# Attention loop of a hybrid transformer layer: the last two value tiles of a step behind the latent scores, and a pair's two copies behind the high halves of groups 0 and 1

## The reference

```python
def block_attention(q, k, v):
    ...
    def one_block(qi):
        s = jnp.einsum('bkgqd,bksd->bkgqs', qi, kt).astype(jnp.float32) * scale
        p = jax.nn.softmax(s, axis=-1).astype(vt.dtype)
        return jnp.einsum('bkgqs,bksd->bkgqd', p, vt)

    o = lax.map(one_block, qb)
    return o.transpose(1, 0, 4, 2, 3, 5).reshape(B, T, Hq * hd)

def reference(x, c, ctx, ...):
        ...
        attn_lat = block_attention(q_lat, jnp.concatenate([k_lat, k_ctx], axis=1),
                                   jnp.concatenate([v_lat, v_ctx], axis=1))
```

## Time and profile before

| | |
|---|---|
| time before, median of 3 runs | 2780.42 us (2778.55 to 2780.79) |
| the profiled execution | 2782.8 us, its span 2781.0 us |
| PE busy over the span | 2698.0 us, 97% |
| DVE busy | 1482.7 us, 53% |
| ACT busy | 627.9 us, 23% |
| POOL busy | 541.7 us, 19% |

### The profile page before, as it was taken

The page is one execution under the profiler, slowest core; times in us unless marked ns, Lnnn a source line. Parts: engine busy times, 40 slices in busy tenths (PEclk is TensorE's granted clock), DMA queues, the critical chain, the costliest instruction groups (busy, mean ns, idle before and its releaser), DMA issues.

```text
span 2781.0 us, 35088 instructions
## 1 busy us (share of the span) xinstructions
PE 2698.0 (97%) x14088; PEld 2202.9 (79%) x14088; DVE 1482.7 (53%) x2349; ACT 627.9 (23%) x1152; POOL 541.7 (19%) x468
## 2 busy tenths in 40 slices
PE   8999999999999999999999989999999999999998
PEld 3888888888888867877777777777778888888887
DVE  6645444344443474167655688867444444444444
ACT  4200000000000044243345688851110000000002
POOL 0065456465420000005420032220000000000001
PEclk9999999999999999999999999999999999999999
DMA  8112112222211122111233100025201111111112
GB/s 294 38 65 65 61 57 73 87 87 91 91 47 37 40 85 66 50 57 62 84 116 107 63 1 1 16 84 161 82 24 53 45 45 53 45 46 52 45 45 76
DMA packets 198289, 187.67 MB, mean 67 GB/s; under 512 B 7645, under 2 KB 149770, under 8 KB 198026
## 3 DMA queue, kind: packets, MB, share of 16 engines
q1 hardware_dynamic: 190160, 171.83, 19.4%
q10 hardware_dynamic: 7994, 13.97, 1.3%
HBM read 161.39 MB, written 24.38 MB: 67 GB/s over the span
## 4 chain that ended last, share of the span: by engine, by line
PE 86%; DVE 6%; ACT 4%; issue 2%; DMA 1%; ACTq 0%; POOL 0%; DVEq 0%; SPq 0%
PE psum L221 26%; PE psum L222 25%; PE psum L223 25%; DVE ptl L1995 2%; PE psum L1876 1%; ACT pth L1945 1%; PE psum L314 1%; ACT prob L1928 1%; PE psum L1500 1%; PE psum L1894 1%; PE psum L1893 1%; PE psum L408 1%; DVE wl L198 1%; PE psum L570 0%; DMA raw<-in_w_out_dram 0%
## 5 line engine op out<-in xcount | busy, mean ns | idle before, releaser
L221 PE MATMUL psum<-nh,wh 128*128 128x512 f32 (+2 forms) x1688 | 627.7, 372 | 1.4 <-DVE wl L198 1.4
L222 PE MATMUL psum<-nl,wh 128*128 128x512 f32 (+2 forms) x1688 | 613.8, 364 | 0.0
L223 PE MATMUL psum<-nh,wl 128*128 128x512 f32 (+2 forms) x1688 | 613.3, 363 | 0.0
L814 ACT ACTIVATE silu_a<-psum 128x512 f32<-128x512 f32 (+1 forms) x110 | 61.2, 556 | 1494.2 <-PE psum L223 1494.2
L196 DVE CAST wh<-raw 128x1024 fp32r<-128x1024 f32 (+1 forms) x173 | 122.4, 708 | 492.9 <-PE psum L223 492.8
L221 PEld LDWEIGHTS psum<-nh,wh 128*128 128x128 f32 (+1 forms) x1688 | 317.3, 188 | 65.9 <-issue 7.1
L222 PEld LDWEIGHTS psum<-nl,wh 128*128 128x128 f32 (+1 forms) x1688 | 317.2, 188 | 52.7 <-issue 4.1
L223 PEld LDWEIGHTS psum<-nh,wl 128*128 128x128 f32 (+1 forms) x1688 | 316.8, 188 | 52.3
L846 DVE SCALAR_TENSOR_TENSOR h<-psum,gates,h 128x512 f32<-128x512 f32 (+1 forms) x400 | 270.9, 695 | 155.9 <-PE psum L223 153.7
L221 PE MATMUL psum<-hidh,wh 128*128 128x512 f32 (+1 forms) x880 | 331.3, 376 | 11.1 <-DVE hidl L830 7.6
L222 PE MATMUL psum<-hidl,wh 128*128 128x512 f32 (+1 forms) x880 | 326.7, 371 | 0.0
(11 more groups left out here) (258 smaller groups left out, 3769.1 us busy)
## 6 DMA issues: line engine op xcount, KB each, us to landing
raw<-in_w_ffn_up_dram SPq DMA_DIRECT2D x88, 512.0 KB, 3.9
mod_part<-in_w_mod_dram SPq DMA_DIRECT2D x96, 256.0 KB, 4.2
raw<-in_w_ffn_down_dram SPq DMA_DIRECT2D x44, 512.0 KB, 3.7
raw<-in_w_in_dram SPq DMA_DIRECT2D x34, 512.0 KB, 3.9
mod_raw<-in_w_mod_dram SPq DMA_DIRECT2D x12, 1024.0 KB, 13.9
gates_saved<-staged ACTq DMA_DIRECT2D x40, 256.0 KB, 2.0
merge_gate<-gates_saved SPq DMA_DIRECT2D x8, 1024.0 KB, 5.2
x_rows<-in_x_dram SPq DMA_DIRECT2D x8, 512.0 KB, 8.1
```

The lines of the kernel that those rows point to most:

```text
L221: pe.matmul(o, hi_w, hi_x, start=first, stop=False)
L222: pe.matmul(o, hi_w, lo_x, start=False, stop=False)
L223: return pe.matmul(o, lo_w, hi_x, start=False, stop=last)
L814: nc.scalar.activation(silu_a[:, c, 0:w], ps[c][:, 0:w], ACT.Silu).then_inc(self.a_free, 1)
```

## The change

On PE, the five value tiles of a step are split in three and two. The first three stay where they were; the last two come behind the latent scores. On ACT, the fold of a pair (in an odd i) comes behind the high halves of groups 0 and 1, no longer ahead of them. No instruction is added or removed, and no wait is written anew.

```diff
             if i >= 4:
 
-                values((i - 4) // 2, range(5, K_TILES) if i % 2 else range(0, 5))
+                tiles = range(5, K_TILES) if i % 2 else range(0, 5)
+                values((i - 4) // 2, tiles[0:3])
             if 2 <= i <= N_STEP:
                 turn(i - 1, (0, 1))
             if i + 2 < N_STEP:
                 score(i + 2, False)
+            if i >= 4:
+                values((i - 4) // 2, tiles[3:5])
             if i in EARLY_MERGE:
...
             if 1 <= i < N_STEP:
                 exp_latent(act, i)
+            if 1 <= i <= N_STEP:
+                high(i - 1, (0, 1))
             if i >= 5 and i % 2 == 1:
                 fold((i - 5) // 2)
-            if 1 <= i <= N_STEP:
-                high(i - 1, (0, 1))
```

## The result

The changed kernel takes 2834.01 us, median of 4 runs (2832.33 to 2834.72), against 2780.61 us for the one before, run beside it (2778.55 to 2781.5). The ratio is 1.0192 with a 95% interval of 1.0175 to 1.021: 53 us slower. The forecast was 2838 us, 41 of it from a new wait and 17 from PE's clock.

What follows compares the result with a forecast made beforehand. A ring of waits among three nearly full engines, PE, DVE and ACT, was taken to set the time. 2780.4 + 41 (new wait) + 17 (PE's clock) = 2838 us; range 2814 to 2862.

Steps and rivals of the forecast that it cites:

- The wait: Odd step, ACT: a new pair's first high half waits for `pv_done`, now behind the latent scores; idle 1.8 us.
- The walk: Odd step, timed from the x2: high half at +3.80 instead of +2.82, DVE's finish at +5.59, 1.42 us later.
- third rival: Odd step: ACT's high halves start at once, only the fold waits; 0.45 us a pair, 2793 us; chance 0.05.
- What a pair costs: Attention steps: a pair takes 9.76 us instead of 8.34, 1.42 more; 29 pairs make 41 us.
- The clock: PE's new idle times halve its clock in 12 of 29 pairs (two in five), 1.4 us each, 17 us; chance 0.52.
- DVE decides: Even step: DVE reaches its low half 1.96 us behind its maxima, at +8.93, later than the high half allows (+8.80).
- the tie with PE: End of the even step: PE is free at +9.76, just when the next x2 follows DVE's low half.
- the clock stays up: PE's clock never falls in the attention steps: 2821.6 us, down to 2816; chance 0.25.
- the clock falls for long: PE's low stretches last 6.7 us: 40 us in place of 17, 2862 us; chance 0.13.
- the high half isn't held: Odd step: ACT's wait is for an earlier pair, so only the fold is held; 13 us, 2793 us; chance 0.05.
- No change: Attention steps: a gain of some 0.3 us a pair against a loss of the same size; chance 0.02.
- Faster: Odd step: earlier transposes save DVE's 0.32 us wait and the new wait is free; 9 us, 2771 us; chance 0.03.

Runs made afterwards that it cites:

- three_buffers: The changed kernel with a third buffer of the turned probabilities for the pairs 0 to 14; 2811.57 us, ratio 1.0124.
- filled: The changed kernel, with the latent scores of odd steps computed a second time behind the value tiles, only then raising their semaphore; 2824.51 us, ratio 1.0167.
- odd_split: The kernel before with ACT's new order and only the odd steps' value tiles split three and two, even steps unsplit; 2835.59 us, ratio 1.0195.
- pe_only: The kernel before with only the PE part of the change, ACT's fold still ahead of the high halves; 2832.85 us, ratio 1.0184.
- odd_one_tile: As odd_split, but with one value tile instead of two behind the latent scores in odd steps; 2836.23 us, ratio 1.0204.
- even_split: The kernel before with only the even steps' value tiles split three and two, ACT in its old order; 2778.39 us, ratio 0.9991.
- rb_behind_even: The kernel before with even steps split three and two, and only the fold's copy of the reciprocals behind the high halves; 2770.04 us, ratio 0.9971.

## Why the prediction was right

By its steps, with the odd step above; +0 is the x2 at 1702.84.

- **The wait.** The high half is released by the value matmul L1894, after 1.75 us (1.8 forecast). three_buffers shows that it is the buffer's wait and not something else at that place.
- **The walk.** The exponential is read out at +1.99 (+1.98), the high half starts at +3.73 (+3.80), DVE's low half at +4.36 (+4.42), the finish at +5.51 (+5.59), the x2 at +5.20 (+5.26), the context scores at +6.12 (+6.23). The last value matmul ends at +3.70 (1706.26 + 0.28), as forecast; ACT follows it by 0.03 and not by 0.10, and with that each later step is a little early. The idle times of PE are 1.50 and 0.51 to 0.66 (1.56 and 0.56). A pair takes 9.6 to 9.8 us (9.76). The releaser is L1894 in the changed kernel too; the prediction called it L1897, but the lines added to the file stand behind it. In its third rival 1704.18 is +3.12, not +3.15, which changes nothing.
- **What a pair costs.** 1.42 forecast; before, pairs were 8.2 to 8.35 us, as the one shown in the earlier trace rows, and are now 9.65 to 9.8: 1.43 more, each kind against its like. In all, without the clock, 52.0 - 13 = 39 us against the 41 of the sum. The difference lies at the loop's end, which the prediction put at nothing: by the distances of filled, which has no fall, the first 28 are 40.9 us longer than before, and the last three, where no latent scores are left, 1.3 us shorter (the last but one 8.30 in place of 9.93).
- **The clock.** Nine falls, each 3.4 us long, against twelve at 3.5; 1.0 to 1.6 us each, pair by pair against filled, 1.4 in the mean as forecast; 12.4 to 13.5 us together against 17. That the clock would fall in part of the pairs and not in all was the weakest step, a choice between bounds of 0 and 40. No row gave the two in five, and kernels with idle times as long or longer had four to six falls in as many pairs (odd_split, pe_only, odd_one_tile), so that nine came near to twelve is partly luck. filled shows that the idle times are the cause, and that the falls have a price.
- **A length that was wrong without harm.** "DVE decides" in the even step rested on 1.96 us as DVE's own length. It was 1.78 (even_split). In the changed kernel the tie with PE, which the prediction also found, holds the step at the same place. In the next pair, at full clock, the low half is at 1722.80, +8.82 in place of +8.93, and PE goes on without an idle time from its value matmuls to the x2, 9.76 us behind that at 1713.98:

```profile
1723.74 0.38 PE L1876 MATMUL psum<-cst,prob 128*128 128x128 f32 x2
```

Of the rivals, *the clock stays up* fell with nine low stretches in the trace, *the clock falls for long* with their length, 3.4 us and not 6.7, *the high half isn't held* with the releaser; what it priced at 0.45 a pair is close to what the first pairs of three_buffers show, 0.33 to 0.49 in most. *No change* fell with the time. *Faster* was right in what ACT and DVE had to give: rb_behind_even collects it, with `pv_done` left where it was.

## What to carry to other kernels

Before moving the work that raises a semaphore, list every wait on that semaphore, those that guard a buffer too: here the visible consumer was moved along, and the costly one was the guard of a double buffer two pairs on, written in another function. A split can be right in one half of a pair and wrong in the other, so try the halves apart. And where a ring of three nearly full engines sets the time, a saving on one of them counts only once the other two can follow; of the two edits that gave 9 us together, neither moved the median alone by more than the measurement can tell, though the even split had shortened the attention steps by 4.7 us in the trace.

## What the runs showed of the hardware that I had not expected

The clock fell in every third pair, with the same idle times of PE (1.50, and 0.51 to 0.66 us behind it) in the two pairs between, where it stayed full. Each fall lasted 3.4 us. The longest idle time is a poor guide. One of 2.81 us had left the clock full before, while in even_split it fell behind one of 1.74 us at the same place of the kernel. At the start of the attention steps it fell behind 2.09 us before and stayed full behind 1.85 us in the changed kernel. The first row is of even_split, the second of the changed kernel:

```profile
1940.95 0.80 PE L221 MATMUL psum<-mh,wo_rest 128*128 128x512 f32 x1 [1.74 <-DVE wo_rest L2131]
```

```profile
1580.18 0.38 PE L1851 MATMUL psum<-kh,qs 128*128 128x256 f32 x1 [1.85 <-ACT prob L1927]
```

pe_only, with one idle time of 2.31 us in each pair, had fewer falls, six, than the changed kernel with its two shorter ones. What filled shows is that with the longer of the two down from 1.50 to 0.58 us there were no falls in these steps. This fits the second of the two sections that the prediction quotes from the Trainium skill, page "TensorE: Matmul & The Clock Gate", "A second HAM failure mode: psum-queue depth-cycling", and speaks against the reading by the first. Why just these pairs had a fall, and others with the same idle times none, is open.

DVE goes through the finish at two speeds, in the kernel before and in pe_only alike. In four pairs it takes 0.60 to 0.61 us from the start of the low half to that of the finish and 0.33 or 0.34 to the next low half; in the next four it takes 0.72 or 0.73 and 0.44 or 0.45, as in the earlier trace rows. A pair of the first kind, in the kernel before:

```profile
1603.87 0.69 DVE L1995 TENSOR_TENSOR ptl<-psum,pth 128x512 fp32r<-128x512 f32 x1 [0.20 <-ACT pth L1945]
1604.48 0.40 DVE L2014 TENSOR_TENSOR att_t<-psum,att_t 64x256 f32<-64x256 f32 x1
1604.81 0.67 DVE L1995 TENSOR_TENSOR ptl<-psum,pth 128x512 fp32r<-128x512 f32 x1
```

Four pairs are one head, and the finish writes rows 0 to 63 of `att_t` for an even head and rows 64 to 127 for an odd one (`rows` at L2014). The slower kind is that of the odd heads. That the rows are the cause is not shown; no run changed them alone.
